# Scores of a windowed attention as two fp32r products in place of one fp32 product

## The reference

```python
def windowed_gqa(q, k, v, sink):
    nb = S // BLOCK
    qb = (q * (HEAD_DIM ** -0.5)).reshape(B, nb, BLOCK, N_KV_HEADS, Q_GROUP, HEAD_DIM)
    ...
    scores = jnp.einsum("bnqhgd,bnkhd->bnhgqk", qb, kb).astype(jnp.float32)
    ...
    scores = scores - slopes * absdist.astype(jnp.float32)
    scores = jnp.where(mask[None, :, None, None, :, :], scores, -jnp.inf)
    m = jnp.maximum(jnp.max(scores, axis=-1, keepdims=True), sink_l)
    p = jnp.exp(scores - m)
    denom = jnp.sum(p, axis=-1, keepdims=True) + jnp.exp(sink_l - m)
    p = (p / denom).astype(v.dtype)
    out = jnp.einsum("bnhgqk,bnkhd->bnqhgd", p, vb)
```

## Time and profile before

| | |
|---|---|
| median of 3 runs | 691.9 us (691.17 to 694.28) |
| the profiled execution | 692.2 us, span of its instructions 690.4 us |
| mean granted TensorE clock | 0.975 |
| TensorE busy | 642.0 us (93% of the span) |
| DVE busy | 351.1 us (51%) |
| ACT busy | 290.2 us (42%) |
| POOL busy | 51.7 us (7%) |
| chain that ended last | PE 73%, DMA 15%, DVE 6%, ACT 4% |

### The profile page before, as it was taken

How to read it: one execution, slowest core, us unless ns; L and a number is a source line. 1 busy time by engine, 2 the same in 40 slices (tenths; PEclk the granted TensorE clock), 3 DMA queues, 4 the chain that set the end, 5 groups by cost and what they waited for, 6 DMA issues and landing times.

```text
span 690.4 us, 10212 instructions
## 1 busy us (share of the span) xinstructions
PE 642.0 (93%) x4037; PEld 484.3 (70%) x4037; DVE 351.1 (51%) x678; ACT 290.2 (42%) x552; POOL 51.7 (7%) x75
## 2 busy tenths in 40 slices
PE   8999899998998785869899999999999999999995
PEld 5979888842542330323389999999788888888884
DVE  4687664731030120110087766657866666666665
ACT  5855562421010110110183655473665555554454
POOL 3100101100010000000049100000000000000001
PEclk9999999999999978899999999999999999999998
DMA  8947308999999999999997333345545555554101
GB/s 342 408 194 259 121 19 326 426 409 425 427 408 422 421 422 419 424 420 421 421 420 268 120 149 122 122 143 188 182 159 183 187 189 196 200 203 185 62 1 61
DMA packets 26286, 180.73 MB, mean 262 GB/s; under 512 B 3184, under 2 KB 3312, under 8 KB 5120
## 3 DMA queue, kind: packets, MB, share of 16 engines
q1 hardware_dynamic: 25488, 177.89, 65.0%
q10 hardware_dynamic: 752, 2.21, 0.8%
HBM read 179.04 MB, written 1.05 MB: 261 GB/s over the span
## 4 chain that ended last, share of the span: by engine, by line
PE 73%; DMA 15%; DVE 6%; ACT 4%; issue 2%; SPq 0%; POOLq 0%; POOL 0%; ACTq 0%; DVEq 0%
PE ps L1542 70%; DMA ring<-stream_dram 14%; PE ps L1545 3%; DVE ring_r L390 1%; ACT single L383 1%; DMA vec<-small_dram 1%; DVE work L1477 1%; ACT work L825 1%; DVE work L1480 1%; ACT work L732 0%; DVE h L1530 0%; ACT turned L830 0%; ACT work_r L821 0%; DVE work L1363 0%; DVE single L1374 0%
## 5 line engine op out<-in xcount | busy, mean ns | idle before, releaser
L1542 PE MATMUL ps<-turned,single 128*128 128x256 f32 (+2 forms) x944 | 231.2, 326 | 1.6 <-ACT work L602 0.8
L1542 PE MATMUL ps<-turned,ring_r 128*128 128x256 f32 (+1 forms) x648 | 179.8, 281 | 0.0
L1542 PEld LDWEIGHTS ps<-turned,single 128*128 128x128 f32 x944 | 156.2, 189 | 18.4 <-issue 2.0
L390 DVE TENSOR_TENSOR ring_r<-ring,single 128x1024 fp32r<-128x1024 f32 (+1 forms) x132 | 160.7, 1240 | 14.8 <-ACT single L383 14.7
L383 ACT ACTIVATE single<-ring 128x1024 fp32r<-128x1024 f32 (+1 forms) x132 | 133.9, 1048 | 0.0
L1542 PEld LDWEIGHTS ps<-turned,ring_r 128*128 128x128 f32 x648 | 121.1, 188 | 0.4
L1542 PE MATMUL ps<-ring,work 128*32 128x512 f32 (+2 forms) x462 | 69.3, 608 | 15.7 <-DMA ring<-stream_dram 13.6
L1542 PEld LDWEIGHTS ps<-single 128*128 128x128 f32 x257 | 39.8, 195 | 34.8 <-issue 22.5
L1542 PE MATMUL ps<-work 128*128 128x128 f32 (+5 forms) x310 | 60.7, 379 | 2.6 <-DVE work L1021 1.8
L1542 PE MATMUL ps<-single,turned 128*128 128x512 f32 (+3 forms) x208 | 59.7, 367 | 1.9 <-DVE turned L1162 1.6
L1542 PE MATMUL ps<-single 128*128 128x512 f32 (+1 forms) x257 | 57.2, 363 | 2.9 <-DVE single L1374 1.9
(11 more groups left out here) (250 smaller groups left out, 698.6 us busy)
## 6 DMA issues: line engine op xcount, KB each, us to landing
ring<-stream_dram SPq DMA_DIRECT2D x146, 1024.0 KB, 11.9
work<-stream_dram SPq DMA_DIRECT2D x12, 1024.0 KB, 14.3
turned_w<-stream_dram SPq DMA_DIRECT2D x4, 1024.0 KB, 15.3
extra<-stream_dram SPq DMA_DIRECT2D x2, 1024.0 KB, 9.9
ring<-stream_dram SPq DMA_DIRECT2D x2, 832.0 KB, 7.8
h<-x_dram SPq DMA_DIRECT2D x2, 512.0 KB, 4.9
gain<-gains_dram ACTq DMA_DIRECT2D x2, 512.0 KB, 8.1
yields<-stream_dram SPq DMA_DIRECT2D x1, 1024.0 KB, 15.1
```

The costliest lines, as they stand in the source:

```text
L390: dve.tensor_tensor(ring_r[:, place, a], ring[:, place, a], w_hi[k % HIGHS][:, a].bitcast(F32), ALU.subtract).then_inc(s["wlo_done"], 1)
L1542: return pe.matmul(o, lhsT, rhs, start=start, stop=stop, **kw)
```

## The change

A query head is no longer taken with its neighbour. Each of the eight heads gets a 128-row block of its own in `q2_split`: the high part of its 64 rows in one half of the rows, the low part in the other half. The high part lies in the rows where the head was computed (even heads in rows 0 to 63, odd ones in 64 to 127). The keys get six blocks in `k2_split`: per key head one with its high part in both halves, and two with its low part in one half and zeros in the other. A score is then two fp32r products with the same stationary block: with the high keys (query high x key high plus query low x key high) and with the low keys (query high x key low).

ACT makes the high parts (`q2_high`, `k2_high`), DVE the low ones (`q2_low`, `k2_low`); both write straight into the rows of the other half where it is needed there, so the two products with the identity and the copies out of PSUM go. The keys are scaled by one DVE instruction of 128 rows. The new blocks lie in `extra`, which held expert weights in block 1; a semaphore of one of its slots is shared with the constants'.

```diff
@@ tiles
-        k2T = cut(4, TOK)
+        k2T = cut(TOK)
+        q2_split = halved(extra_r[:, 0, :], HEADS, TOK)
+        k2_split = halved(extra_r[:, 1, :], 6, TOK)
...
+        def q2_rows(hd, low):
+
+            return slice(HD, P) if hd % 2 != low else slice(0, HD)
+
+        def q2_high(act, c):
+            act.wait_ge(s["q2_sb"], c + 1)
+            for hd in (2 * c, 2 * c + 1):
+                rows = q2_rows(hd, 0)
+                last = act.activation(q2_split[rows, hd, :], q2T[rows, c, :], ACT.Copy)
+            last.then_inc(s["qk_high"], 1)
+
+        def q2_low(dve, c):
+            dve.wait_ge(s["qk_high"], c + 1)
+            for hd in (2 * c, 2 * c + 1):
+                rows = q2_rows(hd, 0)
+                last = dve.tensor_tensor(q2_split[q2_rows(hd, 1), hd, :], q2T[rows, c, :], q2_split[rows, hd, :].bitcast(F32),
+                                         ALU.subtract)
+            last.then_inc(s["qk_low"], 1)
+
+        def k2_high(act, kv):
+            act.wait_ge(s["q2_sb"], CT + 1)
+            rows = slice(kv * HD, (kv + 1) * HD)
+            for other in (kv, 1 - kv):
+                act.activation(k2_split[other * HD:(other + 1) * HD, kv, :], k2T[rows, :], ACT.Copy).then_inc(s["qk_high"], 1)
+
+        def k2_low(dve, kv):
+            dve.wait_ge(s["zpad_done"], 3)
+            dve.wait_ge(s["qk_high"], CT + 2 * kv + 1)
+            rows = slice(kv * HD, (kv + 1) * HD)
+            for odd in (kv, 1 - kv):
+                to = slice(odd * HD, (odd + 1) * HD)
+                last = dve.tensor_tensor(k2_split[to, 2 + 2 * kv + odd, :], k2T[rows, :], k2_split[rows, kv, :].bitcast(F32),
+                                         ALU.subtract)
+            last.then_inc(s["qk_low"], 1)
@@ ACT
             split_high(act, SPLIT1 + 3)
+            q2_high(act, 0)
             split_high(act, SPLIT1 + 4)
+            q2_high(act, 1)
+            q2_high(act, 2)
             split_high(act, SPLIT1 + 5)
-            act.wait_ge(s["zpad_done"], 3)
-            act.wait_ge(s["k2_ps"], 2)
-            for c in range(2):
-                rows = slice((1 - c) * HD, (2 - c) * HD)
-                last = act.activation(k2T[rows, c + 1, :], ps[rows, 1, 0:TOK], ACT.Copy)
-            last.then_inc(s["k2_sb"], 1)
+            q2_high(act, 3)
+            k2_high(act, 0)
+            k2_high(act, 1)
@@ POOL
-            for a in (zp, win, k2T, v2):
+            for a in (zp, win, extra_r[:, 1, 2 * TOK:6 * TOK].bitcast(F32), v2):
@@ DVE
                 if c % 2 == 0:
                     split_low(dve, SPLIT1 + 3 + c // 2)
+                if c:
+                    q2_low(dve, c - 1)
+            q2_low(dve, CT - 1)
             dve.wait_ge(s["k2_ps"], 1)
-            dve.wait_ge(s["zpad_done"], 3)
-            for c in range(2):
-                rows = slice(c * HD, (c + 1) * HD)
-                last = dve.tensor_tensor(k2T[rows, 3 * c, :], ps[rows, 0, 0:TOK], row2[rows, :], ALU.mult)
-            last.then_inc(s["k2_sb"], 1)
+            dve.tensor_tensor(k2T, ps[:, 0, 0:TOK], row2, ALU.mult).then_inc(s["q2_sb"], 1)
+            k2_low(dve, 0)
+            k2_low(dve, 1)
             split_low(dve, SPLIT1 + 5)
@@ TensorE
             values(0)
-            pe.wait_ge(s["k2_sb"], 1)
-            pe.wait_ge(s["z2_sb"], 3)
-            mm(ps[0:HD, 1, 0:TOK], ident[:, HD:P], k2T[:, 3, :], True, True)
-            mm(ps[HD:P, 1, 0:TOK], ident[:, 0:HD], k2T[:, 0, :], True, True).then_inc(s["k2_ps"], 1)
...
             def scores2(u):
                 hd, i = u // 2, u % 2
-                if u == 2:
-                    pe.wait_ge(s["k2_sb"], 2)
+                kv = hd // 4
+                if u % 8 == 0:
+                    pe.wait_ge(s["qk_high"], CT + 2 * kv + 2)
+                    pe.wait_ge(s["qk_low"], CT + kv + 1)
                 if u >= 2:
                     pe.wait_ge(s["nm2_done"], u - 1)
-                mm(ps[:, 2 + u % 2, 0:TOK], q2T[:, hd // 2, i * P:(i + 1) * P], k2T[:, 2 * (hd // 4) + hd % 2, :],
-                   True, True).then_inc(s["s2_ps"], 1)
+                q = q2_split[:, hd, i * P:(i + 1) * P]
+                mm(ps[:, 2 + u % 2, 0:TOK], q, k2_split[:, kv, :], True, False)
+                mm(ps[:, 2 + u % 2, 0:TOK], q, k2_split[:, 2 + 2 * kv + hd % 2, :], False, True).then_inc(s["s2_ps"], 1)
```

More of the change, by code:

```diff
@@ L142, in two_blocks @@
         extra = sb("extra", [P, EXTRA, SLOT])
+        extra_r = nc.alloc_sbuf_tensor_at("extra_r", [P, EXTRA, SLOT], F32R, offset=nc.sbuf_base - 4 * EXTRA * SLOT)
         stat = sb("stat", [P, 160])
@@ L299, in two_blocks @@
         full = [sem(f"slot_full{i}") for i in range(SLOTS)]
-        extra_full = [sem(f"extra_full{i}") for i in range(EXTRA)]
+        extra_full = [const_in, sem("extra_full")]
         full2 = [sem(f"slot2_full{i}") for i in range(SLOTS)]
@@ L308, in two_blocks @@
             sel_done rank_step st_ps st_sb xg_ps xg_act xg_dve gu_ps sg_done ht_done ht_ps hid_done y_ps yh_done yl_done
-            moe_done h2_done z2_ps z2_sb q2_ps q2_sb k2_ps k2_sb v2_ps v2_sb g_ps g_sb zpad_done dp_done
+            moe_done h2_done z2_ps z2_sb q2_ps q2_sb k2_ps qk_high qk_low v2_ps v2_sb g_ps g_sb zpad_done dp_done
             yp_ps yp_sb s2_ps nm2_done e2_done p2_done pt2_ps pt2_sb o2_ps o2_sb sig_done br_ps br_sb
@@ L346, in slot_ready @@
             elif ASIDE_END - EXTRA <= n < ASIDE_END:
-                eng.wait_ge(extra_full[n - (ASIDE_END - EXTRA)], 16)
+                eng.wait_ge(extra_full[n - (ASIDE_END - EXTRA)], 64 if n == ASIDE_END - EXTRA else 16)
             elif is_aside(n):
```

## The result

| | median | lowest to highest | runs |
|---|---|---|---|
| before | 692.39 us | 691.17 to 694.28 | 15 |
| change | 694.86 us | 691.94 to 696.23 | 15 |

The ratio is **1.0035 (1.0025 to 1.0046)**: the change costs 2.4 us (1.7 to 3.2). No change was forecast, with 691.0 to 693.0 as its case; the median lies above that. The profiled execution took 693.61 us, with a span of 691.8.

The account below looks back on a forecast made before the run. The prediction took TensorE to bound the loop, DVE and ACT its start: a start 2.3 us later, 2.3 given back by 12 cheaper scores, sum 0.0, so 691.9 us. Some 85% were to lie from 689.6 to 693.9.

Parts of the forecast that it names:

- TensorE's prices: Attention loop: a score gets 0.19 us cheaper (0.43 to 0.24), so a turn with scores takes 3.55 us, not 3.74.
- DVE beside POOL: Low queries at the start: DVE and POOL take turns, so a half-height subtraction costs 0.78 us, against 0.43 with POOL idle.
- The start on DVE: Ahead of the loop: first score at 384.0 us against 382.38, after a 2.3 us TensorE wait; first maximum 387.2 against 383.24.
- The loop's begin and the values' copies: Loop begins at 387.3 us against 385.97; ACT can start the values' copies at 388.5 against 386.17, 2.3 later.
- The second transpose: Second transpose of probabilities at 395.2 us against 392.91; TensorE, ready at 393.7, waits some 1.5 there.
- the sum: Start delays the second transpose by 2.3 us; the 12 scores behind it give 2.3 back: 0.0, no change.
- rival 3: Clock halves behind the wait before the first score: 0.5 to 2.2 us slower, up to 695.5; beyond 693.0 gets 0.13.
- the forecast's case: Whole kernel at 691.0 to 693.0 us, with either price for DVE and POOL's turns and a small clock loss: chance 0.60.
- Rival 1: At the start, DVE's subtractions cost their time alone (0.45 us each), POOL no hindrance: 690.0 us, chance 0.22.
- Theory 1: Experiments' theory: the wait before the first score costs through the clock, which stays low; TensorE bounds up to the second transpose.
- Theory 2: Experiments' theory: the late start on DVE and ACT alone sets the second transpose; the clock is a bystander.
- Theory 3: Experiments' theory: the loss lies outside the attention.

Follow-up runs that it names:

- the change again: The changed kernel unaltered, measured and profiled a second time: 694.16 us, ratio to the kernel before 1.0035.
- wait filled: The changed kernel with 22 fp32r products that nobody reads in TensorE's wait before the first score: 692.09 us, ratio to before 0.9990.
- wait half filled: The changed kernel with 11 fp32r products that nobody reads in TensorE's wait before the first score: 692.46 us, ratio to before 0.9999.
- POOL later: The changed kernel with POOL's fourth pooling sum held back until the sixth row maximum: 689.59 us, ratio to before 0.9966.
- POOL later, reordered: POOL later, plus one low key part and half of slot 17's split put off on DVE, values' copies behind the next split on ACT: 688.68 us, ratio 0.9947.
- old kernel with a wait: The kernel before, with two unread DVE multiplications that TensorE's identity products and third score wait for: 699.30 us, ratio to before 1.0087.

## Why the prediction was wrong

One sum accounts for all the kernels. The distance from the last value product to the second transpose is taken from the timelines; 11.32 us is that of before, and 2.3 is what the prediction lets the loop's other 12 scores give back. Measured differences are the ratio's, in us.

| kernel | distance | worked out | rest of the span | measured |
|---|---|---|---|---|
| change | 16.87 | 16.87 - 11.32 - 2.3 = +3.3 | +3.2 | +2.4 (1.7 to 3.2) |
| the change again | 17.00 | +3.4 | +3.4 | +2.4 (1.1 to 3.7) |
| wait filled | 13.64 | 0.0 | +0.1 | -0.7 (-1.7 to 0.2) |
| wait half filled | 13.64 | 0.0 | +0.1 | -0.1 (-1.2 to 1.0) |
| POOL later | 11.75 | -1.9 | -1.9 | -2.4 (-3.5 to -1.2) |
| POOL later, reordered | 10.39 | -3.2 | -3.1 | -3.7 (-5.0 to -2.3) |
| old kernel with a wait | 19.16 | 19.16 - 11.32 = +7.8 | +7.7 | +6.0 (3.7 to 8.3) |

The worked-out figures are single executions, up to 1.8 from the measured middles. The fourth column is from the same executions: the span behind the last value product (691.8 - 379.82 = 312.0 for the change), less the 308.8 of before (690.4 - 381.59). It is within 0.2 of the worked-out figure everywhere, so all that stands behind the second transpose moves with it, as was forecast. The profiled executions of the change lose more than its runs do in the middle; whether the low stretch is shorter in some of those is not shown.

Point by point:

- **TensorE's prices: right.** A turn of the loop takes 3.54 (3.55 forecast).
- **DVE beside POOL: right.** 757 ns for a subtraction, forecast 780; with POOL out of the way 421. The sixth ends 0.64 behind the last value product (377.51 + 2.95 - 379.82), forecast 0.51 (382.1 - 381.59).
- **The start on DVE: right.** In the same measure the first score comes after 2.65 (forecast 2.4), the first maximum after 5.70 (5.6), the first exponential after 6.22 (6.1). TensorE waits 2.38 (2.3).
- **The loop's begin and the values' copies: wrong.** 8.65 and 8.89, forecast 5.7 (387.3 - 381.59) and 6.9 (388.5 - 381.59). Here the half clock enters.
- **The second transpose: wrong with it.** 16.87 for 13.6. The wait of 1.5 us that TensorE was to have there is used up: 9.93 us of work at half clock are some 5.0 lost, less 1.5 is 3.5; seen are 3.2.
- **The failed step is the clock: nothing in the sum, and mis-sized in rival 3.** The sum +2.3 - 2.3 has no term for it. The rival's mechanism and place were right: a clock of 0.50 behind the wait before the first score. But it took the length of the low stretch from the earlier trace rows, 3.4 us, so that only the values would stretch, "by up to 1.7, of which the values' copies see" 0.5. It lasted 10.2 us, three times as long, and the gate chunk behind the values stretched too. A second fall, which the rival also priced, did not come, nor did the low keys take turns with POOL (420 ns each). That 694.86 lies below the rival's upper end of 695.5 is therefore luck. What it put at 0.5 from the first fall costs 3.2, and the forecast's case, which allowed "a small clock loss", could not hold it.
- **The trace of before already had a stretch of this length.** The earlier trace rows is one of the shortest of the low stretches in block 1 there (3.4 to 10.2 us). TensorE was busy for 9.68 of 10.2 us at half clock in the longest, much as in the change. Priced by it, half of 10.2 less the wait of 1.5, the first fall would have cost some 3.6 (an estimate). Its row, with the one ahead of it and the columns of the earlier trace rows:

```profile
238.00:242.50 4.50, 2.00 (x20) 0.32 (x16) 0.00 (x0) 0.00 (x0) 0.00 (x0) 1.00 1.03 428
242.50:252.70 10.20, 9.68 (x50) 4.19 (x46) 3.42 (x10) 1.46 (x3) 0.00 (x0) 0.50 1.01 419
```

- **What spoke against the rival did not hold.** The prediction set against it that at the earlier trace rows weights arrive late, while here products stand between two short waits. The old kernel with a wait alone shows that this place falls as well. And in the trace of before, single waits shorter than the 2.3 us that was forecast stand ahead of both falls: the idle 1.8 us of the earlier trace rows are two waits of 0.38 and 1.42, and ahead of 242.5 are two of 1.16 and 1.34, with products between them (TensorE's timeline, first at the earlier trace rows, then ahead of 242.5):

```profile
208.99 1.06 PE L1542 MATMUL ps<-ring,work 128*32 128x512 f32 x8 [0.38 <-DMA ring<-stream_dram]
211.47 1.78 PE L1542 MATMUL ps<-ring,cst 128*128 128x512 f32 x2 [1.42 <-DMA ring<-stream_dram]
```

```profile
239.78 1.06 PE L1542 MATMUL ps<-ring,work 128*32 128x512 f32 x8 [1.16 <-DMA ring<-stream_dram]
242.18 1.66 PE L1542 MATMUL ps<-ring,work 128*32 128x512 f32 x8 [1.34 <-DMA ring<-stream_dram]
```

- **One reading of the old trace was too strong.** The prediction says that DVE and ACT already set the second transpose there. It stands 0.51 us behind the start of its score (392.91 - 392.40); where the first one waits for nothing, that is 0.43 (389.32 - 388.89). TensorE lost 0.08 at most, so the two paths ended almost together. The sum does not hang on it.
- **Rival 1 is what POOL later turned out to be.** Subtractions at their time alone were to put the values' copies 0.4 later and to give 690.0; the second transpose came 0.43 later, and the time was 689.59.

Theory 1 stands. Theory 2 falls with the half filled wait: the same start on DVE, and the second transpose 3.2 us sooner. Theory 3 falls with it too, as nothing outside this place was altered. **What stays open** is what sets the length of the low stretch: 10.2 us twice here, and 13.7 in the old kernel with a wait (from 384.0 to 397.7), although TensorE was busy almost all that time; it was not tried. The kernel alone does not set it: around 240 us of block 1, which no run alters, a low stretch lasts 10.2 us in the traces of before and of the change, 3.4 in that of POOL later (241.0 to 244.4), and 13.7 in that of the change once more:

```profile
239.40:253.10 13.70, 12.44 (x58) 4.65 (x62) 3.42 (x10) 1.46 (x3) 0.00 (x0) 0.50 1.01 422
```

Nor do these cases say at what length a wait begins to bring a fall. At the edited place 2.38 and 2.04 us did, 1.03 and 0.49 did not; in block 1 a fall stands behind 1.42, and another behind 1.16 and 1.34 with products between them.

## What to carry to other kernels

A wait of TensorE is not only its own length: ask what follows if the clock falls behind it, and price that with the longest low stretch that the trace shows anywhere (10.2 us in the one of before, not the 3.4 that was taken), over all work that stands there, before calling the wait covered. Filling half of the wait with products of no use brought back the lost time here; taking away its cause, POOL's work beside DVE's short instructions with two inputs in SBUF, and putting off what the first turns do not need, brought the gain too. Where stages ahead of the edited place vary between executions, compare places by their distance from a common instruction.

## What was not expected of the hardware

- The clock stayed at 0.50 with TensorE busy for 9.93 of 10.2 us, and for all of 12.6 us in the old kernel with a wait, and only then rose; the trace of before has the same at 242.5. The Trainium skill (TensorE: Matmul & The Clock Gate, "Part 1: The HAM clock gate") says that the clock falls after idleness and comes back once the array has been busy; the fall behind a wait agrees with these rows, the return came later than the one at the earlier trace rows had led the prediction to take.
- Of the four low keys (L488), two are written into the rows that they are read from and two into the other half's. All four cost 418 to 423 ns: the shift across the halves cost nothing there.
